# A mixture-of-experts stage in half-precision parts: the gate's clip moves to ScalarE, and items of 128 columns split all four down chunks

## What is computed

```python
gu = x_blk @ w_gate_up[e] + b_gate_up[e]
g = jnp.minimum(gu[:, :D_EXPERT], SWIGLU_LIMIT)          # 7.0
u = jnp.clip(gu[:, D_EXPERT:], -SWIGLU_LIMIT, SWIGLU_LIMIT)
act = (u + 1.0) * (g * jax.nn.sigmoid(SWIGLU_ALPHA * g))  # alpha 1.702
return act @ w_down[e] + b_down[e]
```

## Time and profile before

| | us |
|---|---|
| median of the timed runs | 1878.76 |
| the profiled run | 1882.29 |
| its span, first to last instruction | 1880.5 |
| PE busy | 1800.9 (96%) |
| DVE busy | 1402.1 (75%) |
| ACT busy | 1231.7 (65%) |
| q1 (weights and other direct DMAs) | 64.9% of 16 engines |
| high parts, L1869, x336, 1907 ns each | 639.0 |
| low parts, L1996, x336, 2283 ns each | 767.2 |
| float32 down matmuls of the narrow items, L2254 (PE) | 150.2 |

### The profile page before, as it was taken

How to read it: one execution, slowest core, us unless ns; L and a number is a source line. 1 busy time by engine, 2 the same in 40 slices (tenths; PEclk the granted TensorE clock), 3 DMA queues, 4 the chain that set the end, 5 groups by cost and what they waited for, 6 DMA issues and landing times.

```text
span 1880.5 us, 53844 instructions
## 1 busy us (share of the span) xinstructions
PE 1800.9 (96%) x21814; PEld 1650.7 (88%) x21814; DVE 1402.1 (75%) x2678; ACT 1231.7 (65%) x1649; POOL 411.4 (22%) x304
## 2 busy tenths in 40 slices
PE   8999998998987999999999999999999999999996
PEld 7777765666876999999999999999999999999996
DVE  5553637775258888888888899999889877757755
ACT  6565327873114777777777788877777776656654
POOL 4000000001003212111112332333122224434433
PEclk9999999999988999999999999999999999999998
DMA  5211101004438988889999999999999999999994
GB/s 153 56 44 39 30 24 45 2 1 142 142 120 295 369 293 308 304 302 320 325 320 322 328 313 343 344 336 345 373 375 365 372 372 374 377 375 372 362 370 134
DMA packets 251408, 479.07 MB, mean 255 GB/s; under 512 B 17312, under 2 KB 38096, under 8 KB 251264
## 3 DMA queue, kind: packets, MB, share of 16 engines
q1 hardware_dynamic: 231040, 443.59, 64.9%
q0 software_dynamic: 20256, 33.94, 7.6%
HBM read 466.96 MB, written 47.19 MB: 273 GB/s over the span
## 4 chain that ended last, share of the span: by engine, by line
PE 50%; issue 6%; DVE 6%; ACT 4%; DMA 2%; DVEq 0%; SPq 0%; POOLq 0%; ACTq 0%; POOL 0%
PE E_p_d L2254 9%; PE E_p_g L2242 5%; PE E_p_g L2245 5%; PE E_p_g L2244 5%; PE E_p_u L2242 5%; PE E_p_u L2245 5%; PE E_p_u L2244 5%; PE E_p_d L2242 3%; PE E_p_d L2245 3%; PE E_p_d L2244 3%; DVE E_w_lo L1996 3%; DMA E_w_st<-in_w_down 2%; PE E_p_t L2180 2%; PE E_p_t L2195 2%; ACT E_w_hi L1869 2%
## 5 line engine op out<-in xcount | busy, mean ns | idle before, releaser
L1996 DVE SCALAR_TENSOR_TENSOR E_w_lo<-E_w_st,E_w_hi 128x2048 f16<-128x2048 f32 x336 | 767.2, 2283 | 31.7 <-ACT E_w_hi L1869 30.5
L1869 ACT ACTIVATE E_w_hi<-E_w_st 128x2048 f16<-128x2048 f32 x336 | 639.0, 1907 | 20.3 <-PEq L1325 16.8
L2242 PE MATMUL E_p_u<-E_x_hi,E_w_hi 128*128 128x128 f16 (+9 forms) x2048 | 366.9, 222 | 1.5 <-DVE E_w_lo L1996 1.4
L2244 PE MATMUL E_p_g<-E_x_lo,E_w_hi 128*128 128x128 f16 (+9 forms) x2048 | 366.9, 222 | 0.5 <-issue 0.5
L2242 PE MATMUL E_p_g<-E_x_hi,E_w_hi 128*128 128x128 f16 (+9 forms) x2048 | 366.9, 222 | 0.0
L2245 PE MATMUL E_p_g<-E_x_hi,E_w_lo 128*128 128x128 f16 (+9 forms) x2048 | 366.9, 222 | 0.0
L2245 PE MATMUL E_p_u<-E_x_hi,E_w_lo 128*128 128x128 f16 (+9 forms) x2048 | 366.8, 222 | 0.0
L2244 PE MATMUL E_p_u<-E_x_lo,E_w_hi 128*128 128x128 f16 (+9 forms) x2048 | 366.8, 222 | 0.0
L1799 POOL DMA_INDIRECT out<-E_y_rows,E_idx_out x66 | 152.6, 2312 | 488.0 <-ACT E_y_rows L1887 467.1
L2242 PE MATMUL E_p_d<-E_a_hi,E_w_hi 128*128 128x160 f16 (+6 forms) x1024 | 210.6, 231 | 6.9 <-DVE E_a_lo L2090 3.5
L2245 PE MATMUL E_p_d<-E_a_hi,E_w_lo 128*128 128x160 f16 (+6 forms) x1024 | 210.5, 231 | 0.0
(11 more groups left out here) (419 smaller groups left out, 3487.2 us busy)
## 6 DMA issues: line engine op xcount, KB each, us to landing
E_w_st<-in_w_gate_up SPq DMA_DIRECT2D x130, 2048.0 KB, 13.5
E_w_st<-in_w_down SPq DMA_DIRECT2D x64, 2048.0 KB, 18.7
A_w_st<-in_w_in SPq DMA_DIRECT2D x20, 512.0 KB, 4.0
A_x_rows<-in_x SPq DMA_DIRECT2D x8, 512.0 KB, 7.9
C_x_res<-in_x SPq DMA_DIRECT2D x8, 512.0 KB, 4.7
x_rows<-C_x SPq DMA_DIRECT2D x8, 512.0 KB, 5.2
out<-C_x SPq DMA_DIRECT2D x8, 512.0 KB, 5.9
h_rows<-C_h SPq DMA_DIRECT2D x8, 512.0 KB, 4.5
```

Source lines behind the costliest of these rows:

```text
L1869: act.activation(w_hi[r][:], staged(c), ACT.Copy, scale=SW).then_inc(hi_s if c < NG else down_hi_s, 1)
L1996: dve.scalar_tensor_tensor(out=w_lo[r][:], in0=staged(c), scalar=SW, in1=w_hi[r][:], op0=ALU.mult, op1=ALU.subtract, accum_out=total[:, c: ...
L2242: pe.matmul(o_, wh, hi[:, k, 0:w], start=h == 0 and k == 0, stop=False, skip_group_check=True)
L2244: pe.matmul(o_, wh, lo[:, k, 0:w], start=False, stop=False, skip_group_check=True)
```

## The change

1. The gate's clip goes to ScalarE. `clip_gate` is gone. `silu(j)` first does two Relu activations out of PSUM with a factor of -1 and a bias of limit less gate bias, which gives limit minus the gate, cut at zero; Silu then takes `ALPHA * LIMIT` less that, with the constant in a one-column tile `top`. The bias tile is prepared accordingly.
2. Items of 128 columns split all four down chunks (`n_split` is 4 where it was 2), so the tile `a_slim` is gone, and slot 5 is released by splits of VectorE, not by the end of the down matmuls.
3. `split_lo` takes the small maximum always ahead of the low part, and `fold` waits for the low parts' semaphore instead of the maxima's.

```diff
         def n_split(w):
-            return (NP if w > HALVES else NP // 2) if halves(w) else 0
+            return NP if halves(w) else 0
...
                     def silu(j):
+                        if j == 0:
+                            act.wait_ge(bias_s, i + 1)
+                        act.wait_ge(gu_mm, NG * i + 2 * j + 1)
+                        if j >= 2:
+                            act.wait_ge(act_s if halves(w) else a_s, NP * i + j - 1)
+                        for h in range(2):
+                            ins = act.activation(gate[j % 2][:, h, 0:w], p_g[j % 2][:, h, 0:w], ACT.Relu,
+                                                 bias=bias[:, 2 * j + h:2 * j + h + 1], scale=-1.0)
+                        ins.then_inc(gate_s, 1)
                         act.wait_ge(gate_s, FREE + NP * i + j + 1)
-                        act.activation(gate[j % 2][:, :, 0:w], gate[j % 2][:, :, 0:w], ACT.Silu, scale=ALPHA / S1
-                                       ).then_inc(silu_s, 1)
+                        act.activation(gate[j % 2][:, :, 0:w], gate[j % 2][:, :, 0:w], ACT.Silu, scale=-ALPHA / S1,
+                                       bias=top[:]).then_inc(silu_s, 1)
...
                         if fast and j % 2 == 1 and j >= n_split(w):
                             act.sem_inc(down_lo_s, 2)
-                            if halves(w):
-                                act.sem_inc(down_hi_s, 2)
...
-            def split_lo(k, c, r, first=False):
...
+            def split_lo(k, c, r):
                 dve.wait_ge(hi_s if c < NG else down_hi_s, k)
-                if first:
-                    largest()
+                dve.tensor_reduce(peak[:, c:c + 1], w_hi[r][:, :, 0:1], AX.XY, ALU.max,
+                                  apply_absolute_value=True).then_inc(peak_s if c < NG else down_peak_s, 1)
                 dve.scalar_tensor_tensor(out=w_lo[r][:], in0=staged(c), scalar=SW, in1=w_hi[r][:],
                                          op0=ALU.mult, op1=ALU.subtract,
                                          accum_out=total[:, c:c + 1]).then_inc(lo_s if c < NG else down_lo_s, 1)
-                if not first:
-                    largest()
...
-            def fold(k, wide):
+            def fold(i, w):
+                k, wide = i + 1, halves(w)
                 dve.wait_ge(fold_s, 2 * k)
-                dve.wait_ge(peak_s, NG * k)
+                dve.wait_ge(lo_s, NG * k)
+                if wide:
+                    dve.wait_ge(down_lo_s, NP * i + n_split(w))
...
-                    dve.tensor_scalar(bias[:, 0:8], of_expert[:, 0:8], S1, None, ALU.mult)
+                    dve.tensor_scalar(bias[:, 0:8], of_expert[:, 0:8], -S1, S1 * LIMIT, ALU.mult, ALU.add)
...
-                        for h in range(2):
-                            ins = dve.tensor_scalar(gate[j % 2][:, h, 0:w], p_g[j % 2][:, h, 0:w],
-                                                    bias[:, 2 * j + h:2 * j + h + 1], S1 * LIMIT, ALU.add, ALU.min)
-                        ins.then_inc(gate_s, 1)
...
                     for c in range(NG):
                         j = c // 2
-                        if c % 2 == 0:
-                            clip_gate(j)
-                        else:
+                        if c % 2 == 1:
                             clip_up(j)
                             product(j)
```

More of the change, by code:

```diff
@@ L1578, in stage_e @@
             a_hi, a_lo = (at(n, [P, KT, CHUNK], F16, (o + 4 * i) * KIB) for i, n in enumerate(("a_hi", "a_lo")))
-            a_slim = at("a_slim", [P, KT, P], F32, o * KIB)
-            a_slim_hi, a_slim_lo = (at(n, [P, KT, P], F16, (o + 4 + 2 * i) * KIB)
-                                    for i, n in enumerate(("a_slim_hi", "a_slim_lo")))
         rows = at("rows", [P, NB, D], F32, 144 * KIB)
@@ L1593, in stage_e @@
         warm = at("warm", [P, 1], F32, 202 * KIB + 704)
+        top = at("top", [P, 1], F32, 202 * KIB + 640 + 32)
         out_of = at("out_of", [P, 4], F32, 202 * KIB + 512)
@@ L1635, in n_split @@
         def n_split(w):
-            return (NP if w > HALVES else NP // 2) if halves(w) else 0
+            return NP if halves(w) else 0
         def parts_of(w):
-            return (a_hi, a_lo) if w > HALVES else (a_slim_hi, a_slim_lo)
+            return a_hi, a_lo
         def ring(c, w):
@@ L1822, in run @@
                 pool.wait_ge(cleared, 2)
+                pool.memset(top[:], ALPHA * LIMIT).then_inc(warm_s, 1)
+                pool.wait_ge(warm_s, 1)
                 pool.memset(warm[:], 0.0).then_inc(warm_s, 1)
-                pool.wait_ge(warm_s, 1)
+                pool.wait_ge(warm_s, 2)
                 pool.memset(gates[:], 0.0).then_inc(gates_s, 1)
@@ L1937, in next_hi @@
                         split_hi(c, c)
-                    act.wait_ge(warm_s, i + 1)
+                    act.wait_ge(warm_s, i + 2)
                     act.activation(warm[:], warm[:], ACT.Silu).then_inc(warm_s, 1)
@@ L1986, in _ @@
         def _(dve):
-            def split_lo(k, c, r, first=False):
-                def largest():
-                    dve.tensor_reduce(peak[:, c:c + 1], w_hi[r][:, :, 0:1], AX.XY, ALU.max,
-                                      apply_absolute_value=True).then_inc(peak_s if c < NG else down_peak_s, 1)
+            def split_lo(k, c, r):
                 dve.wait_ge(hi_s if c < NG else down_hi_s, k)
-                if first:
-                    largest()
+                dve.tensor_reduce(peak[:, c:c + 1], w_hi[r][:, :, 0:1], AX.XY, ALU.max,
+                                  apply_absolute_value=True).then_inc(peak_s if c < NG else down_peak_s, 1)
                 dve.scalar_tensor_tensor(out=w_lo[r][:], in0=staged(c), scalar=SW, in1=w_hi[r][:],
@@ L2036, in run @@
                     dve.memset(peak[:, NG:NC], 1.0).then_inc(down_peak_s, 2)
-                    split_lo(1, 0, 0, True)
+                    split_lo(1, 0, 0)
                     gate_parts(2 * BATCH)
@@ L2047, in run @@
                     for c in range(1, RI):
-                        split_lo(c + 1, c, c, True)
+                        split_lo(c + 1, c, c)
                 def body(i, w):
@@ L2079, in product @@
                             dve.wait_ge(d_mm, NP * i)
-                        to = up[j % 2][:, :, 0:w] if halves(w) and w > HALVES else (
-                            a_slim if halves(w) else a_f)[:, 2 * j:2 * j + 2, 0:w]
+                        to = up[j % 2][:, :, 0:w] if halves(w) else a_f[:, 2 * j:2 * j + 2, 0:w]
                         dve.scalar_tensor_tensor(out=to, in0=up[j % 2][:, :, 0:w],
@@ L2087, in activated_lo @@
                         dve.wait_ge(act_hi_s, NP * i + j + 1)
-                        src = up[j % 2][:, :, 0:w] if w > HALVES else a_slim[:, 2 * j:2 * j + 2, 0:w]
+                        src = up[j % 2][:, :, 0:w]
                         hi, lo = parts_of(w)
@@ L2108, in body @@
                             if c == NG - RI:
-                                fold(i + 1, False)
+                                fold(i, w)
                                 dve.wait_ge(fold_s, 2 * (i + 2))
@@ L2112, in body @@
                     if halves(w):
-                        if n_split(w) < NP:
-                            dve.sem_inc(down_peak_s, NP - n_split(w))
-                        fold(i + 1, True)
+                        fold(i, w)
                         dve.wait_ge(fold_s, 2 * (i + 2))
@@ L2119, in body @@
                         x_part(i + 1, 1, w)
-                        split_lo(NG * (i + 1) + 1, 0, 0, True)
+                        split_lo(NG * (i + 1) + 1, 0, 0)
                         for g in range(2, 2 * blocks(w)):
@@ L2123, in body @@
                         for c in range(1, RI):
-                            split_lo(NG * (i + 1) + c + 1, c, c, True)
+                            split_lo(NG * (i + 1) + c + 1, c, c)
                     elif fast:
@@ L2278, in down @@
                         else:
-                            whole_chunk(NG + j, p_d[j % 2], a_slim if halves(w) else a_f, k0, k1)
+                            whole_chunk(NG + j, p_d[j % 2], a_f, k0, k1)
                     def down_lo_sy(j):
```

6 lines of the change are left out of this document (2 added, 4 removed).

## The result

The change makes the kernel slower. In the same session the kernel before took 1880.05 us (median of 6, 1877.91 to 1881.97) and the changed one 1885.69 (median of 6, 1883.50 to 1888.72): ratio 1.0034, 95% interval 1.0021 to 1.0046, or +5.6 us. The forecast was +5.7.

The account below looks back on a forecast made before the run. TensorE bounds the widest and 112-column items; after the change a ring of waits bounds those of 128. Terms -2.4 (144, 136), +9.0 (128), -0.5 (96) give +6.1, less 0.4 is +5.7: 1884.5 us, range 1875.5 to 1891.

Parts of the forecast that it names:

- The ring: Items of 128: closed loop of waits, slot 5's landing to slot 5's next landing, 38.3 us against 36.8 now, +9 us.
- high part of chunk 10: First step in items of 128: slot 5 lands and ScalarE writes this part, then the maximum, 2.1 us.
- VectorE to the end of chunk 2's low part: Second step: VectorE goes on to the next item's chunk 2, the third release of slot 0, 14.5 us.
- slot 0's issue to slot 5's landing: Last step: slots 0, 1 and 5 come one behind the other, 21.5 us; wrong if within 20.5.
- Rival A: Items of 128: ring does not close, VectorE's round (34.7 us work, 2.3 waits) gives 37.0; total 1875, chance 0.22.
- Part 1 at 144: Gate's clip moved to ScalarE, items of 144 columns: gains all 1.0 us in which TensorE is idle.
- At 136: Clip's gain in two items of 136 columns: 2 x 0.7 = 1.4 us, then slot 5's landing binds; bounds 0.7 to 4.0.
- the lengths that the forecast named as signs: Item lengths that would show the forecast right: 39.7 us at 136 columns, 39.9 at 144.
- At 112 columns: Clip's gain in items of 112 columns: nothing, since TensorE is busy 179.03 of 179.20 us.
- At 96: Items of 96 columns: products come earlier, but TensorE waits for weight landings instead; gain 0.5 us, bounds 0 to 5.
- Rival C: Items of 128: passage takes 22.5 us, +13 or 1891; a clock drop, up to 6.7 us an item, put here; chance 0.12.
- Rival D: Items of 128: Relus delay high parts and ScalarE bounds with 35.1 us of work; total 1877, no change; chance 0.06.

Follow-up runs that it names:

- experiment 9: Changed kernel with 48 further matmuls on TensorE during its wait for the last activation low part, in items of 128 columns: 1888.87 us, ratio 1.0028 to before.
- experiment 3: Changed kernel with one SyncE line moved, so slot 5 is issued ahead of slots 0 and 1 in items of 128 columns and wider: 1873.77 us, ratio 0.9964.
- experiment 7: Changed kernel with SyncE issuing slot 0, then 5, then 1 in items of 128 columns and wider: 1880.16 us, ratio 0.9998 to before.
- experiment 8: Changed kernel plus one VectorE reduction per item of 128, inside the ring (1895.39 us, ratio 1.0082) or outside it (1887.29 us, ratio 1.0038).
- experiment 1: Changed kernel with only the clip on ScalarE: items of 128 split two down chunks again, as before the change. 1876.69 us, ratio 0.9981 to before.
- experiment 2: Changed kernel with the gate's clip back on VectorE, all four down chunks of items of 128 still split: 1889.41 us, ratio 1.0055 to before.
- experiment 5: Changed kernel with slot 5 issued ahead of slots 0 and 1 and the gate's clip back on VectorE: 1889.09 us, ratio 1.0032 to before.
- experiment 4: Changed kernel with the last activation high and low parts written ahead of chunk 11's, in items of 128 columns alone: 1899.86 us, ratio 1.0114 to before.

## Why the prediction was right, point by point

- **The ring** (forecast 38.3 us an item): 38.0 measured. Its terms: high part of chunk 10, 2.1 forecast, 2.02 measured (1382.14 to 1384.16); VectorE to the end of chunk 2's low part, 14.5 and 14.4; issue, 0.2 and 0.17; slot 0's issue to slot 5's landing, 21.5 and 2.94 + 18.4 = 21.3. From slot 0's issue to slot 5's landing the other items of 128 show 21.3 to 21.4, the first 22.2. The mechanism is right. That its sum for six items, +9.0 - 0.4 = 8.6, comes so near the measured +8.3 is in part luck: a ring of 38.0 us gives about +7, and +6.6 is what experiment 9 has, where the clock did not fall; most of the rest is the sixth item, 39.6 us, in which it fell (see the last section). The forecast had the ring 0.3 us an item too long and the clock at nothing. Experiments 3, 7 and 8 show it by cutting it at its DMA leg in two ways and by lengthening it at its VectorE leg.
- **Rival A's 37.0** for an item whose ring does not close: experiments 3 and 7, in which ScalarE does not wait for slot 5, take 36.8. The round's work was 34.7 forecast, 34.5 measured.
- **Part 1 at 144**: -1.0 forecast, -1.4 measured. I had read TensorE's 1.0 idle us of the stage as all there was to win. **At 136**: -1.4 forecast, -0.7 measured: the first of the two items gained nothing, since ScalarE's wait for slot 5 grew:

```profile
ACT E_w_hi L1869 <- DMA E_w_st<-in_w_down: 1.7, 1, 1.7
```

  It was 1.1. So the lengths that the forecast named as signs, 39.7 at 136 columns and 39.9 at 144, came out as 40.3 and 39.7, and 40.1, 40.1 and 40.0.
- **At 112 columns**: 0 forecast, -1.5 measured. This term was wrong. The items went from 35.82 to 35.54 us with the clip (experiment 1) and stayed at 35.83 without it (experiment 2). "Busy 179.03 of 179.20" was read as no room, but TensorE's busy time fell too, to 177.70: a short wait stood inside it. The row of weight loads has it (total, times, longest, before):

```profile
PEld E_p_d L2254 <- DVE E_a_f L2082: 1.1, 5, 0.2
```

  Five items, five waits, for the last pair's product. In the third of these items VectorE ends it at 1607.15, and that is when TensorE goes on with the last slices of the down chunks, 26.2 us into the item; in after it goes on at 26.0, where the product has been done for 0.6 us, and the item is 0.3 us shorter from there on. With the clip on ScalarE the row is gone (after, experiment 1), without it it is there (experiment 2: 1.2 us, five times).
- **At 96**: -0.5 forecast, +0.9 measured. TensorE waited for the stream, as said, and lost more by it than I took. TensorE's waits there in after (total, times, longest), where the earlier trace rows had 4.9 for the products and, of weight loading, 3.9 for landings:

```profile
PE E_p_d L2245 <- DMA E_w_st<-in_w_down: 5.0, 4, 2.0
...
PE E_p_d L2245 <- DVE E_a_f L2077: 0.6, 1, 0.6
```

  The wait for products is nearly gone and that for landings took its place. In experiment 3, whose stream is ahead, the first four of these items take 34.5 to 35.0 us and in after 34.6 to 37.6. The 37.6 is not the stream alone. Behind its wait of 2.0 us for a landing the clock fell for 3.4 us, and TensorE was busy 35.0 us in it, 1.7 more than in its neighbours; in the next two items it waited 0.7 us for landings instead of 2.0, so part of that came back. No forecast term had this fall; in the kernel before, the clock stays up through this stage.
- The misses at 144, 136, 112 and 96 (-0.4, +0.7, -1.5, +1.4) cancel, so the total is nearer than its terms: that is luck.
- **Rival C** priced a fall of the clock at up to 6.7 us an item. The passage took 21.3 us and not C's 22.5, but the clock fell in two of six items, for some 1.5 us each; the first of the two came back, the second did not within the stage (below). **Rival D** does not describe after, where ScalarE stands idle for slot 5's landing in all six items, 0.8 to 1.4 us. Whether ScalarE would bound with the ring cut is not settled by experiment 5, which gives VectorE 2.0 us an item as it takes 2.4 off ScalarE.
- On the rule that sends relu and min to VectorE (the Trainium skill, "ScalarE: Activation LUTs", "Rules for kernel authors"): here the measured balance decides against it. The clip on ScalarE is 3.6 us faster than on VectorE (experiment 1), though dearer by the instruction (359 ns in after's items of 128 against 343), since VectorE is the fuller engine.

## What to carry to other kernels

Before work is moved onto half-idle engines, look for the ring that it closes: a buffer's release, the issue, the transfers queued ahead, the consumer, and the way back to the release. Its length is the sum of its legs, whatever each engine's busy share is, and the order of the queue can cut it without any faster instruction: here one moved line turned +5.6 us into -6.8. Two waits that stand within a microsecond of each other hide one another, so test the edits together as well as one by one, and follow each gain to the end of the program, where a stream of weights may take it back.

## What else the runs showed

TensorE's clock fell behind some waits and not behind others. In the changed kernel's fourth 128-column item TensorE waited 2.9 us, from 1425.3 to 1428.2, and the granted clock was 1.00 through the wait and for another 1.1 us of work; then it was 0.51, the lower of the two levels (1.2 of 2.4 GHz), for 3.4 us:

```profile
1425.30:1428.20 2.90, 0.03 (x1) 0.04 (x2) 2.90 (x7) 2.68 (x4) 2.59 (x2) 1.00 1.05 386
1429.30:1432.70 3.40, 3.40 (x34) 3.16 (x32) 3.40 (x6) 3.40 (x6) 0.00 (x0) 0.51 1.04 385
```

Behind waits of 2.8 us in the second and third item it stayed at 1.00. Length alone does not decide it: elsewhere it fell behind waits of 1.5 us (experiment 9, a 136-column item) and 1.7 us (experiment 2, likewise), and stayed up behind others of the same length. The fourth item took 39.4 us, and the next one 36.7:

```profile
1397.60:1437.00 39.40, 36.40 (x598) 35.74 (x597) 35.65 (x62) 35.14 (x47) 12.79 (x7) 0.96 1.01 355
1437.00:1473.70 36.70, 34.71 (x598) 34.34 (x597) 33.63 (x58) 33.39 (x46) 11.44 (x7) 1.00 1.02 358
```

Together they are 76.1, two rings of 38.05: while TensorE was slow, the ring's other engines and the transfers went on, so the next round of TensorE found them ready. In experiment 9, without the lower clock, the same two take 75.7. So here the loss was given back by the next item.

The sixth item's was not. The next stage, 112 columns, is the one where TensorE is the bound, and it takes the same time whatever came before it (177.7 in after and in experiments 1, 3, 4 and 9 alike):

```profile
1473.70:1513.40 39.70, 36.56 (x599) 35.91 (x598) 35.98 (x63) 35.34 (x49) 12.78 (x7) 0.96 0.99 350
```

The same item takes 38.4 us in experiment 9. Whether these 1.3 us are found again in the 96 stage, where TensorE waits for landings, is not shown: the totals of the two kernels cannot be told apart, and the clock fell at other places in each. What decides behind which wait it falls stays open too.
